# Routing tokens to experts through memory, in a two-layer encoder trunk with a top-2 expert layer

## The reference

```python
def swiglu(h, w_gate, w_up, w_down):
    return (jax.nn.silu(h @ w_gate) * (h @ w_up)) @ w_down

def moe_swiglu(h, w_router, w_gate, w_up, w_down):
    logits = (h @ w_router).astype(jnp.float32)
    top_vals, top_idx = lax.top_k(logits, TOP_K)
    top_w = jax.nn.softmax(top_vals, axis=-1)
    combine = jnp.sum(jax.nn.one_hot(top_idx, N_EXPERTS, dtype=jnp.float32) * top_w[..., None], axis=-2)
    y = jnp.zeros_like(h)
    for e in range(N_EXPERTS):
        y = y + combine[..., e:e + 1] * swiglu(h, w_gate[e], w_up[e], w_down[e])
    return y
```

## Time and profile before

| What | us |
|---|---|
| median of three runs | 1575.85 |
| lowest, highest | 1575.54, 1576.43 |
| time of the profiled execution | 1575.58 |
| its span, first to last instruction | 1573.7 |
| PE busy | 1550.5 |
| DVE busy | 1217.1 |
| ACT busy | 1010.2 |
| POOL busy | 3.5 |
| moved by DMA | 444.32 MB, 282 GB/s over the span |

### The profile page before, as it was taken

The page is one execution under the profiler, slowest core; times in us unless marked ns, Lnnn a source line. Parts: engine busy times, 40 slices in busy tenths (PEclk is TensorE's granted clock), DMA queues, the critical chain, the costliest instruction groups (busy, mean ns, idle before and its releaser), DMA issues.

```text
span 1573.7 us, 18320 instructions
## 1 busy us (share of the span) xinstructions
PE 1550.5 (99%) x7426; PEld 1286.7 (82%) x7426; DVE 1217.1 (77%) x1030; ACT 1010.2 (64%) x974; POOL 3.5 (0%) x9
## 2 busy tenths in 40 slices
PE   9999999999999999999999999999999999999997
PEld 8888788887988788888888887887888888888885
DVE  5666656556655688988988888888888888898886
ACT  6655543344565377767767776776776776776774
POOL 0000000000000000000000000000000000000000
PEclk9999999999999999999999999999999999999999
DMA  9633555455633469999999999999998999999992
GB/s 355 207 114 112 199 196 187 148 191 177 196 113 121 134 236 364 382 325 347 378 343 336 375 348 336 373 349 340 366 374 310 368 377 320 363 374 338 351 365 104
DMA packets 192633, 444.32 MB, mean 282 GB/s; under 512 B 7288, under 2 KB 12936, under 8 KB 192544
## 3 DMA queue, kind: packets, MB, share of 16 engines
q1 hardware_dynamic: 190944, 440.37, 78.7%
q10 hardware_dynamic: 1296, 2.12, 0.5%
q0 software_dynamic: 304, 0.60, 0.1%
HBM read 442.01 MB, written 1.05 MB: 282 GB/s over the span
## 4 chain that ended last, share of the span: by engine, by line
PE 95%; DVE 3%; issue 1%; DMA 1%; ACT 1%; SPq 0%; ACTq 0%; DVEq 0%
PE A L401 20%; PE A L403 19%; PE A L402 19%; PE DN L401 8%; PE DN L403 8%; PE DN L402 8%; PE T L1600 2%; PE T L1641 2%; PE DN L1607 2%; PE DN L1457 1%; PE T L403 1%; PE T L402 1%; PE T L401 1%; DMA xs<-in_x 1%; DVE wlo L376 1%
## 5 line engine op out<-in xcount | busy, mean ns | idle before, releaser
L376 DVE TENSOR_TENSOR wlo<-raw,whi 128x2048 fp32r<-128x2048 f32 (+2 forms) x335 | 754.5, 2261 | 176.9 <-ACT whi L369 176.1
L369 ACT ACTIVATE whi<-raw 128x2048 fp32r<-128x2048 f32 (+2 forms) x335 | 632.0, 1895 | 243.1 <-PE A L403 147.2
L401 PE MATMUL A<-whi,heTh 128*128 128x512 f32 x672 | 272.3, 405 | 1.2 <-DVE heTl L1188 1.2
L403 PE MATMUL A<-whi,heTl 128*128 128x512 f32 x672 | 262.5, 391 | 0.0
L402 PE MATMUL A<-wlo,heTh 128*128 128x512 f32 x672 | 261.8, 390 | 0.0
L376 DVE TENSOR_TENSOR wlo_more<-raw,whi_more 128x2048 fp32r<-128x2048 f32 x84 | 192.2, 2289 | 37.2 <-ACT whi_more L369 36.8
L369 ACT ACTIVATE whi_more<-raw 128x2048 fp32r<-128x2048 f32 x84 | 161.1, 1918 | 35.9 <-PE A L403 19.9
L401 PE MATMUL A<-whi,hTh 128*128 128x512 f32 (+2 forms) x448 | 174.2, 389 | 4.5 <-DVE hTl L861 1.8
L403 PE MATMUL A<-whi,hTl 128*128 128x512 f32 (+2 forms) x448 | 170.0, 379 | 0.0
L402 PE MATMUL A<-wlo,hTh 128*128 128x512 f32 (+2 forms) x448 | 169.9, 379 | 0.0
L401 PEld LDWEIGHTS A<-whi,heTh 128*128 128x128 f32 x672 | 126.2, 188 | 29.1 <-issue 3.4
(11 more groups left out here) (289 smaller groups left out, 1811.2 us busy)
## 6 DMA issues: line engine op xcount, KB each, us to landing
raw<-in_moe_w_gate SPq DMA_DIRECT2D x112, 1024.0 KB, 7.1
raw<-in_moe_w_up SPq DMA_DIRECT2D x112, 1024.0 KB, 7.4
raw<-in_moe_w_down SPq DMA_DIRECT2D x112, 1024.0 KB, 6.9
raw<-in_w_in SPq DMA_DIRECT2D x22, 1024.0 KB, 5.2
raw<-in_dense_w_down SPq DMA_DIRECT2D x11, 1024.0 KB, 4.9
raw<-in_dense_w_gate SPq DMA_DIRECT2D x10, 1024.0 KB, 5.1
raw<-in_dense_w_up SPq DMA_DIRECT2D x10, 1024.0 KB, 5.2
raw<-in_w_out SPq DMA_DIRECT2D x8, 1024.0 KB, 5.0
```

What stands on the lines that cost most here:

```text
L369: nc.scalar.activation(split_slot(u, e)[0][:, :n], raw[:, u % R, :n], ACT.Copy).then_inc(hi_done, 1)
L376: nc.vector.tensor_tensor(lo[:, :n], raw[:, u % R, :n], hi[:, :n].bitcast(F32), ALU.subtract).then_inc(lo_done, 1)
L401: nc.tensor.matmul(o, hi, wh, start=start, stop=False)
L403: return nc.tensor.matmul(o, lo, wh, start=False, stop=stop)
```

## The change

Two tables in memory are added, `tokens_by_slot` (row e x 128 + slot holds that token; 8 x 128 rows and 512 spare ones) and `outputs_by_slot`.

- Early on POOL clears `zero`, and after the load of unit 10 SP writes 4 MB of zeros from it over `tokens_by_slot`.
- After `routed` POOL computes for each token, for its first and its second expert, the row in the table: 20 operations on 128x16 elements or fewer, each behind a wait for the one before except one. It then scatters the rows of `xn` with four indirect transfers of 128 rows of 4 KB. 25 more operations give the rows for the way back and the weights.
- In group 2 of each expert ACT waits for the scatter and issues the load of the next expert's 128 rows to `he` (512 KB). PE transposes them (`turn_tokens`) where the halves of `gather` stood. Only expert 0 still gathers, with `pick`.
- In group 0 of experts 1 to 7 ACT waits for both halves of `oe` and stores it to `outputs_by_slot`. The spreads, the `cw` transposes and the adds of the experts 0 to 6 are gone. In expert 7 POOL waits for the last of these stores and fetches the rows of each token with four indirect transfers, and DVE multiplies them by the weights and adds them to `xs` in groups 3 to 6 (`add_back`). Expert 7 itself still goes through `cw` and `spread`.
- The expert weights are laid out in memory so that a unit is one run of 1 MB, 8 KB for each partition; before, a partition had four runs of 2 KB (gate, up) or two of 4 KB (down).
- The semaphores of the norms are merged into three.

The core of the diff (left out: buffers, constants and semaphores added, the merged semaphores, the second turn):

```diff
@@ SP @@
+                if u == 10:
+                    sp.wait_ge(zero_set, 1)
+                    sp.dma_start(by_slot[0:SPARE, :].rearrange("(e p) d -> p e d", p=P),
+                                 zero[:].unsqueeze(1).broadcast_to([P, NE, D])).then_inc(zero_landed, 16)
...
-                gate = moe_w_gate[0, bass.ds(e, 1)].rearrange("a (k p) n -> p (a k) n", p=P)
-                up = moe_w_up[0, bass.ds(e, 1)].rearrange("a (k p) n -> p (a k) n", p=P)
-                dn = moe_w_down[0, bass.ds(e, 1)].rearrange("a (k p) n -> p (a k) n", p=P)
+                gate, up, dn = (w[bass.ds(e, 1)].rearrange("a u p k n -> p (a u) k n")
+                                for w in (moe_w_gate, moe_w_up, moe_w_down))
...
@@ ACT @@
+                    if l == 0 and f == 0:
+                        act.wait_ge(zero_landed, 16)
                     nc.scalar.activation(pT[:, f % 2, :], T[f % 2][:], ACT.Copy).then_inc(probs_T_out[l], 1)
...
                     ahead.to(u + (5 if j < EG else 3))
+                    if n == 0 and e and j == 0:
+                        act.wait_ge(oe_act, e)
+                        act.wait_ge(oe_dve, e)
+                        act.dma_start(rows_out[(e - 1) * P:e * P, :], oe[:]).then_inc(rows_landed_out, 16)
+                    if following and j == 2:
+                        act.wait_ge(scattered, 16 * 2 * NB)
+                        act.dma_start(he[:], by_slot[(e + 1) * P:(e + 2) * P, :]).then_inc(he_landed, 16)
...
-                    if j == 1:
-                        act.wait_ge(cw_T, n + 1 + e)
+                    if j == 1 and spreads_here(n, e):
+                        act.wait_ge(cw_T, spreads(n, e))
                         nc.scalar.activation(cwT[:], T[1][:, :SEQ], ACT.Copy).then_inc(cw_out, 1)
...
                 ahead.to(base + EU + S)
+                if n == 0 and e:
+                    act.wait_ge(rows_landed_out, 16 * e)
                 act.wait_ge(unit_used, base + EU + e * EU)
                 nc.scalar.activation(oe[:, 0:N], DN[0][:], ACT.Copy).then_inc(oe_act, 1)
@@ DVE @@
+            def add_back(b, r):
+
+                dve.wait_ge(back_landed, 16 * 2 * NB)
+                dve.wait_ge(weights_known, 1)
+                dve.wait_ge(x_added[1], 4 + 2 * b + r)
+                nc.vector.scalar_tensor_tensor(xs[:, b, :], back[b][:, r, :], back_w[:, r, b:b + 1], xs[:, b, :],
+                                               ALU.mult, ALU.add).then_inc(x_added[1], 1)
...
-                    if carried and j == 0:
-                        add_spread(0, DN, oe_full, 4 * (e - 1) + 1, x_added[1])
...
-                    if following and j == EG - 2:
-                        select(0, n + 1, e, e + 1)
+                    if n == 0 and e == NE - 2 and j == EG - 2:
+                        weigh(0, NE - 1, 1)
...
-                    if carried and j == 0:
-                        add_spread(1, DN, oe_full, 4 * (e - 1) + 3, x_added[1])
+                    if n == 0 and e == NE - 1 and 3 <= j < 3 + 2 * NB:
+                        add_back((j - 3) // 2, (j - 3) % 2)
...
-            head(0, UM, 0, 0, first)
+            choose(0, 0, 0)
+            first.to(UM + S)
+            for i in range(2):
+                tokens_low(i, 0, 0)
@@ PE @@
+            def turn_tokens(i, e):
+
+                pe.wait_ge(he_landed, 16 * e)
+                for kk in range(4):
+                    k = 4 * i + kk
+                    last = nc.tensor.transpose(T[i][:, kk * P:(kk + 1) * P], he[:, k * P:(k + 1) * P], ident)
+                last.then_inc(gathered, 1)
...
-                    if carried and j == 0:
-                        pe.wait_ge(oe_act, e)
-                        pe.wait_ge(oe_dve, e)
-                        spread(0, DN, oe_full)
...
-                    if j == 1:
+                    if j == 1 and spreads_here(n, e):
+                        pe.wait_ge(weighed, NB * spreads(n, e))
                         for b in range(NB):
                             last = nc.tensor.transpose(T[1][:, b * P:(b + 1) * P], cw[:, b], ident)
                         last.then_inc(cw_T, 1)
                     if following and j == EG:
-                        gather(1, n + 1, e)
+                        turn_tokens(1, e + 1)
...
-                    if carried and j == 0:
-                        pe.wait_ge(x_added[1], 4 + 4 * (e - 1) + 2)
-                        spread(1, DN, oe_full)
                     if following and j == EG - 1:
                         pe.wait_ge(ff_lo[1], EG * n + EG - 2 + e * EG)
-                        gather(0, n + 1, e)
+                        turn_tokens(0, e + 1)
                     if j:
-                        if carried and j == 1:
-                            pe.wait_ge(x_added[1], 4 + 4 * e)
+                        if n == 0 and e and j == 1:
+                            pe.wait_ge(oe_act, e)
+                            pe.wait_ge(oe_dve, e)
@@ POOL @@
+            pool.memset(zero[:], 0.0).then_inc(zero_set, 1)
...
+            def of_turn(r, values, out):
+
+                done(pool.tensor_scalar(chosen[:], rank[:], float(r), None, ALU.is_equal))
+                settle()
+                done(pool.tensor_tensor(part[:], chosen[:], values[:], ALU.mult))
+                settle()
+                for w in (4, 2):
+                    done(pool.tensor_tensor(part[:, :, :w], part[:, :, :w], part[:, :, w:2 * w], ALU.add))
+                    settle()
+                done(pool.tensor_tensor(out, part[:, :, 0], part[:, :, 1], ALU.add))
+                settle()
+
+            pool.wait_ge(routed, 1)
+            done(pool.tensor_scalar(fit[:], pos[:], float(P), None, ALU.is_lt))
+            done(pool.tensor_tensor(row[:], pos[:], table(K_ROW), ALU.add))
+            settle()
+            for r in range(2):
...
+                of_turn(r, row_in, row_sum[:])
+                done(pool.tensor_tensor(row_sum[:], row_sum[:], spare, ALU.add))
+                settle()
+                done(pool.tensor_copy(slot_in[:, r, :], row_sum[:]))
+                settle()
+            pool.wait_ge(zero_landed, 16)
+            for r in range(2):
+                for b in range(NB):
+                    pool.indirect_dma_start(by_slot, bass.IndirectOffsetOnAxis(ap=slot_in[:, r, b:b + 1], axis=0),
+                                            xn[:, b, :], None).then_inc(scattered, 16)
...
+            pool.sem_inc(weights_known, 1)
+            pool.wait_ge(scattered, 16 * 2 * NB)
+            pool.wait_ge(rows_landed_out, 16 * (NE - 1))
+            for b in range(NB):
+                for r in range(2):
+                    pool.indirect_dma_start(back[b][:, r, :], None, rows_out,
+                                            bass.IndirectOffsetOnAxis(ap=slot_out[:, r, b:b + 1], axis=0)
+                                            ).then_inc(back_landed, 16)
```

More of the change, by code:

```diff
@@ L221, in trunk @@
         xT = place("xT", [P, KD + KD * SEQ], F32, o_g)
+        o_qT = used[0]
         qT = place("qT", [P, HEADS, SEQ], F32)
+        back = [place(f"back{b}", [P, 2, D], F32, o) for b, o in enumerate((o_pj, o_qT))]
         o_kT = used[0]
@@ L226, in trunk @@
         gfin = place("gfin", [P, D], F32, o_kT)
+        o_bg = used[0]
         bg = place("bg", [P, 2, N], F32)
+        he = place("he", [P, D], F32, o_bg)
         o_sx = used[0]
@@ L264, in trunk @@
         combc = place("combc", [P, NB], F32, o_sx + 1568)
+        fit, row, row_in, row_out, kept, kept_comb, chosen, part = (
+            place(f"slot_{n}", [P, NB, NE], F32, o_sx + 2048 + 64 * i) for i, n in enumerate(
+                ("fit", "row", "row_in", "row_out", "kept", "kept_comb", "chosen", "part")))
+        row_sum = place("row_sum", [P, NB], F32, o_sx + 2560)
+        back_w = place("back_w", [P, 2, NB], F32, o_sx + 2592)
+        slot_in = place("slot_in", [P, 2, NB], I32, o_sx + 2624)
+        slot_out = place("slot_out", [P, 2, NB], I32, o_sx + 2656)
         A = [ctx.enter_context(nc.psum_tensor(f"A{i}", [P, N], F32)) for i in range(4)]
@@ L1608, in spread, with expert @@
                                      start=True, stop=True).then_inc(full, 1)
-            def expert(base, n, e, following, carried):
+            def expert(base, n, e, following):
                 def products(u, h, bank):
@@ L1713, in _, with done, settle, table @@
             pool.wait_ge(gfin_landed, 16)
+            own = [0]
+            def done(ins):
+                own[0] += 1
+                ins.then_inc(pool_own, 1)
+            def settle():
+                pool.wait_ge(pool_own, own[0])
+            def table(k):
+                return cst[:, k:k + NB * NE].rearrange("p (b e) -> p b e", b=NB)
+            def of_turn(r, values, out):
[8 more added lines that the diff above has]
+                settle()
@@ new lines, in _ @@
+            pool.wait_ge(routed, 1)
[3 more added lines that the diff above has]
+            for r in range(2):
+                spare = cst[:, K_SPARE + r * NB:K_SPARE + (r + 1) * NB]
```

(16 more changed lines are left out.)

136 lines of the change are left out of this document (88 added, 48 removed).

## The result

| | before | after |
|---|---|---|
| median of 4 runs, us | 1575.84 (1575.54 to 1576.43) | 1539.12 (1538.87 to 1539.30) |
| profiled execution, us | 1575.58 | 1538.87 |
| its span, us | 1573.7 | 1536.8 |
| first product of the first expert | 567.14 | 566.62 |
| start of the last expert's spread | 1562.59 | 1525.77 |

The ratio is 0.9766, with a 95% interval of 0.9750 to 0.9783. The forecast of 1540.0 was 0.9 us too high. Of the 36.9 us by which the span shrank, 36.3 lie between the first expert's first product and the start of the last spread (959.15 against 995.45), 0.5 ahead of it, and 0.1 behind.

A forecast was written before the change was run, and what follows sets the result against it. PE's queue was taken as the bound. Seven handovers at 5.11 us save 35.8, the head 0.3, other terms 0: -36 from 1575.85 gives 1540 us, range 1536 to 1555, forecast case 1537 to 1543 at 0.68.

The forecast's parts named there:

- rival 3: Expert stage: the DMA becomes the bound; at 353 GB/s an expert takes 127.7 us, +19 us, 1595; chance 0.05.
- The sum per handover: PE between two experts: spreads, `cw` transposes and both gather halves together save 5.11 us, seven times 35.8 us.
- first half: Gather at j = 6 of each handover: replacing it by four transposes saves PE 1.34 us.
- second half: Gather at j = 7 of each handover: replacing it saves 0.13 us, where its own length promises 1.34.
- the uncovered chain to `aTl`: PE transposes, ACT `aTh`, DVE `aTl` before the down products: 2.01 us bare; durations alone would promise 44 us, 8.5 more.
- The idle time beside it: PE idle about 1.2 us once per handover, released by DVE `aTl`; more than 2 us would prove the forecast wrong.
- The head: Expert 0's start: gather waits for two `pick`s without `cw`s, -0.5 us unless POOL's new operations take it back; -0.3 taken.
- The scatter: POOL's chain, issues and landing after `routed`: done about 590, free until 604, cost 0; bounds 568 to 621.
- rival 1: Scatter late, POOL's operations each queue behind a `wlo`: up to 17 us once, 1541 to 1557; chance 0.14.
- the upper bound: POOL's 20 operations after `routed` each wait for one `wlo` of 2.29 us: 46 us, scatter done at 621.
- The zeros: 4.2 MB stored after unit 10 delay unit 11 by 10.4 or 27 us; cost 0 or some 9 us, 0 taken.
- The layout: Expert weights in 1 MB runs, 8 KB per partition: nothing waits for them, gain 0; helps against a DMA bound.

The follow-up runs named there:

- the high half first: Changed kernel, at each expert's last group the eight first-down-tile products needing only the activations' high half made before the four with the low half: 1533.34 us.
- twice the chain: Changed kernel with POOL's chain between the choice of slots and the first scatter issue made twice over: 1542.90 us.
- four times the chain: Changed kernel with POOL's chain between the choice of slots and the first scatter issue made four times over: 1554.88 us.

## Why the prediction was right

**What bounds the stage.** PE's queue, as read from the earlier trace rows. The DMA did not become the bound at 377 GB/s (rival 3). The Trainium skill (DMA: Bandwidth & Descriptors, Where 436 GB/s comes from) puts the limit for loads from HBM at about 358 GB/s per core; by that figure an expert would have taken an estimated 126 us, and it took 119.8, so the trace disagrees. The page gets the figure as half of what a memory stack gives two cores, and here one core runs.

**The sum per handover.** 5.11 predicted; from the period 125.0 - 119.8 = 5.2. The experiments confirm it in three parts: first half 1.30 for 1.34, second half 0.13 for 0.13, and the rest 26.7 for 25.5 + 0.5. No run parts the spreads (3.42) from the `cw` transposes (0.22), and the 0.7 us that the rest gave beyond its sum are not explained. The term that kept the forecast from being 8.5 us too low was the uncovered chain to `aTl`; the earlier trace rows had shown it to the hundredth (2.01 us). The idle time beside it in the prediction, about 1.2 us, was mis-sized, at no cost to the sum: of the bare 1.41 the four new transposes take 0.44, which leaves the 0.97 measured.

**The head.** -0.3 taken, -0.5 measured: the first estimate of -0.5 was right, since POOL took nothing back. DVE's `wlo` took its 2.29 us beside POOL's chain as before.

**The scatter.** The cost of 0 came true (rival 1 did not). "Done about 590" fits too, but by luck: its parts were wrong and their errors met. POOL in the changed kernel:

```profile
559.53 0.33 POOL L1807 TENSOR_SCALAR slot_fit<-pos 128x16 f32<-128x16 f32 x1 [51.20 <-DVE flag L1209]
559.78 0.21 POOL L1808 TENSOR_TENSOR slot_row<-pos,cst 128x16 f32<-128x16 f32 x1
560.07 2.29 POOL L1812 TENSOR_TENSOR slot_row_in<-slot_row,cst 128x16 f32<-128x16 f32 x1
562.43 2.14 POOL L1815 TENSOR_TENSOR slot_row_in<-slot_row_in,slot_fit 128x16 f32<-128x16 f32 x1
...
570.95 0.18 POOL L1820 CAST slot_in<-row_sum 128x2 int32<-128x2 f32 x1
...
576.49 2.07 POOL L1825 DMA_INDIRECT tokens_by_slot<-xn,slot_in  x1 [0.30 <-issue]
```

The chain took 11.6 us, three of its twenty operations over 2 us and the others 0.2 to 0.3; the 590 of the prediction had left some 25 us for it. Three `wlo` ran on DVE in that time, and the three slow operations began while one was running:

```profile
560.00 4.50 DVE L405 TENSOR_TENSOR wlo<-raw,whi 128x2048 fp32r<-128x2048 f32 x2
564.42 2.15 DVE L1247 SCALAR_TENSOR_TENSOR heTl<-T,gcol,heTh 128x128 fp32r<-128x128 f32 x8
567.05 2.29 DVE L405 TENSOR_TENSOR wlo_more<-raw,whi_more 128x2048 fp32r<-128x2048 f32 x1 [0.48 <-ACT whi_more L398]
```

So what the upper bound had wrong was the count: twenty waits of a `wlo` each cannot fall into a time in which only a few `wlo` run. The issues were mis-sized: 1.5 us in the mean, and 7 for the four with their gaps, where 2.2 had been taken from the earlier trace rows. The landing, too. This trace does not show it, but in the seven experiments whose scatter had the weights streaming beside it the medians are 9.5 to 11.4 us, against the 3.4 of an `out` store. In two of them the issues stand as in the changed kernel (the last at 576.8, for the 576.5 above); their longest landings, 13.1 (the high half first) and 14.9 us (the second half of the gather back on PE), put the last row in memory at 590 to 592 if they are the last issue's, as in the runs that show ACT's release; that is the estimate for the changed kernel, whose ACT asked for the rows at 597.5. Errors of opposite sign met: a shorter chain, longer issues and a longer transfer. In the expectation for twice the chain the same landing error was not covered, and that one failed.

**The zeros.** 0, as forecast. The store took 20.2 us from issue to landing, unit 11 was issued at 32.47 for 32.01, and PE's waits between 20 and 120 us are the same three as before. One more sign was off in what to look for: the DMA share stayed at 0.98 and did not fall below it. Of the two figures for the delay of unit 11, 10.4 and 27 us, no run here says which was nearer.

**The layout.** 0, as forecast and as measured on its own. That it "helps" against a bound on the DMA shows only in ACT's waits, 17.5 us without it and none with it.

## What to carry to other kernels

Before counting a removed operation at its own length, look for the operand that the next one waits for: a place in the same kernel where the cover is missing already shows how much is left. Then the order of the products decides; where an operand is split into a high and a low half, start with what needs only the high one. And price a transfer from a row with the same load beside it: the scatter landed in 3.7 us in a quiet stretch and in 9.5 to 11.4 in busy ones (medians).

## What the runs showed of the hardware that was not expected

Small POOL operations (128x16) take 0.2 to 0.3 us, but about 2.1 to 2.3 us where they begin while a DVE `wlo` of 2.3 us is running. In the run with four times the chain DVE stood still from 601.8 to 618.1, waiting for ACT, and POOL ran whole passes of nine operations in 2.6 us (603.30 to 605.91); the pass from 586.26 to 596.73, beside four `wlo` on DVE, took 10.5, with four slow operations. Two of the operations of either pass:

```profile
589.25 2.08 POOL L1798 TENSOR_TENSOR slot_part<-slot_chosen,slot_row_in 128x16 f32<-128x16 f32 x1
...
591.97 2.13 POOL L1803 TENSOR_TENSOR row_sum<-slot_part 128x2 f32<-128x2 f32 x1
...
604.25 0.22 POOL L1798 TENSOR_TENSOR slot_part<-slot_chosen,slot_row_in 128x16 f32<-128x16 f32 x1
...
605.11 0.19 POOL L1803 TENSOR_TENSOR row_sum<-slot_part 128x2 f32<-128x2 f32 x1
```

```profile
618.08 0.69 DVE L1266 TENSOR_TENSOR aTl<-T,aTh 128x512 fp32r<-128x512 f32 x1 [16.29 <-ACT aTh L803]
```

This is the rule that the prediction cited from the Trainium skill (SBUF — State Buffer, Who interferes with whom), and the trace agrees in its direction; one slow operation came with each `wlo`, three of twenty in the chain, not all. DVE's `wlo` kept its 2.3 us.

The issue of an indirect transfer followed suit: 0.95 to 1.11 us each while DVE stood still, up to 3.2 beside its work (in the run with the old layout). That the landing grows from 3.7 us to 9.5 and more because of the weights beside it is the likeliest reading: ACT's stop had brought the weights to a halt in the one run, where the 262 GB/s from 609 to 617 are no more than the scatter's own 2.1 MB, while 427 GB/s went through from 595 to 605.4 with the chain twice over. But no run changed the load alone; that stays open.
